# Hybrid decoder layer, one core: value sums of sparse attention in another matmul form, the C matrix of S5 in another bank, x's second read later in the queue

## What is computed

```
for block n of 128 tokens:
    p_cmp = softmax(q @ k_cmp^T ...);     o_cmp = p_cmp @ v_cmp          # 63 compressed blocks
    idx = top_k(sum of p_cmp over heads and overlaps)                    # from the ungated p_cmp
    p = softmax(q @ k_sel^T ...);         o_sel = p @ v_sel
    p = softmax(q @ k_win^T ...);         o_win = p @ v_win              # window of 512
    o = g[..., 0:1] * o_cmp + g[..., 1:2] * o_sel + g[..., 2:3] * o_win
s5:   bu = B u;  states = scan;  y = Re(C states) + D u;  gelu, glu
stick-breaking attention (4 heads)
merged = gate0 * (o_a @ w_br_nsa) + gate1 * (o_b @ w_br_s5) + gate2 * (o_c @ w_br_sb)
x = x + merged @ w_out
x = x + conv_ffn(rms_norm(x), w_up, conv_w, conv_b, w_down)
```

## Time and profile before

| what | us |
|---|---|
| median of 3 runs (1495.3 to 1495.51) | 1495.47 |
| the profiled execution | 1493.83 |
| its span | 1492.1 |
| PE busy in it | 1416.8 (95%) |
| VectorE busy | 673.0 (45%) |
| ScalarE busy | 355.2 (24%) |
| GpSimd busy | 471.1 (32%) |

### The profile page before, as it was taken

One profiled execution on the slowest core, in us unless ns is written; L12 is line 12 of the kernel. 1 busy time (PEld: TensorE's weight loads), 2 busy tenths in 40 slices (PEclk: granted clock), 3 DMA queues, 4 the chain that ended last, 5 costly groups with the idle time before them and its releaser, 6 DMA issues.

```text
span 1492.1 us, 18380 instructions
## 1 busy us (share of the span) xinstructions
PE 1416.8 (95%) x7437; PEld 1159.1 (78%) x7437; DVE 673.0 (45%) x1053; ACT 355.2 (24%) x621; POOL 471.1 (32%) x240
## 2 busy tenths in 40 slices
PE   5799799999999899999999979999999999999998
PEld 4688467799887667777778868788888888888887
DVE  5896665525453553444445231532323232364641
ACT  5311544400101134344401010421111111231110
POOL 4324002234622110111133333334434343444542
PEclk9999999999989899999999999999999999999999
DMA  7411101031101000000012041321111111141122
GB/s 181 45 29 42 43 1 29 15 76 54 36 19 52 15 22 1 19 18 18 1 36 53 29 159 53 127 72 43 49 49 42 56 42 56 42 156 56 43 72 98
DMA packets 126821, 76.44 MB, mean 51 GB/s; under 512 B 39312, under 2 KB 113424, under 8 KB 126736
## 3 DMA queue, kind: packets, MB, share of 16 engines
q1 hardware_dynamic: 126752, 75.46, 18.0%
HBM read 66.93 MB, written 8.52 MB: 51 GB/s over the span
## 4 chain that ended last, share of the span: by engine, by line
PE 88%; DVE 5%; ACT 3%; issue 1%; DMA 1%; POOL 0%; SPq 0%; ACTq 0%; DVEq 0%; POOLq 0%
PE ps L642 23%; PE ps L643 23%; PE ps L644 23%; PE ps L1123 4%; PE ps L1153 3%; PE ps L1137 2%; PE ps L875 1%; PE ps L892 1%; PE ps L905 1%; DMA raw<-in_w_out 1%; PE ps L657 1%; PE ps L1081 1%; ACT arena L1269 1%; PE ps L1100 1%; DVE hTl L2009 1%
## 5 line engine op out<-in xcount | busy, mean ns | idle before, releaser
L554 POOL TENSOR_TENSOR wh<-raw,zero 128x1024 fp32r<-128x1024 f32 (+2 forms) x93 | 188.1, 2022 | 988.3 <-PE ps L644 950.4
L642 PE MATMUL ps<-hTh,wh 128*128 128x512 f32 x1008 | 402.8, 400 | 3.9 <-ACT arena L1344 3.1
L643 PE MATMUL ps<-hTl,wh 128*128 128x512 f32 x1008 | 395.8, 393 | 0.0
L644 PE MATMUL ps<-hTh,wl 128*128 128x512 f32 x1008 | 395.6, 392 | 0.0
L557 POOL TENSOR_TENSOR wl<-raw,wh 128x1024 fp32r<-128x1024 f32 (+2 forms) x93 | 257.0, 2763 | 7.3
L642 PEld LDWEIGHTS ps<-hTh,wh 128*128 128x128 f32 x1008 | 191.7, 190 | 43.4 <-ACT arena L1344 3.5
L644 PEld LDWEIGHTS ps<-hTh,wl 128*128 128x128 f32 x1008 | 191.1, 190 | 41.1
L643 PEld LDWEIGHTS ps<-hTl,wh 128*128 128x128 f32 x1008 | 191.7, 190 | 37.8
L642 PE MATMUL ps<-wh,hTh 128*128 128x512 f32 (+2 forms) x512 | 179.9, 351 | 7.5 <-POOL wl L557 7.5
L643 PE MATMUL ps<-wl,hTh 128*128 128x512 f32 (+2 forms) x512 | 179.6, 351 | 0.0
L644 PE MATMUL ps<-wh,hTl 128*128 128x512 f32 (+2 forms) x512 | 179.5, 351 | 0.0
(11 more groups left out here) (331 smaller groups left out, 1596.7 us busy)
## 6 DMA issues: line engine op xcount, KB each, us to landing
raw<-in_w_in SPq DMA_DIRECT2D x35, 512.0 KB, 3.9
raw<-in_w_up SPq DMA_DIRECT2D x32, 512.0 KB, 4.0
raw<-in_w_down SPq DMA_DIRECT2D x16, 512.0 KB, 3.7
merged<-in_x SPq DMA_DIRECT2D x8, 512.0 KB, 7.2
raw<-in_w_out SPq DMA_DIRECT2D x8, 512.0 KB, 3.7
merged<-in_x SPq DMA_DIRECT2D x2, 2048.0 KB, 10.3
x_keep<-merged SPq DMA_DIRECT2D x2, 2048.0 KB, 10.1
conv<-x_keep SPq DMA_DIRECT2D x1, 2048.0 KB, 8.1
```

Of the source, the lines that this page charges most:

```text
L554: eng.tensor_tensor(wh[:, p, 0:n], raw[:, p, 0:n], zero1[:, 0:1].broadcast_to((P, n)), ALU.add).then_inc(s_hi[0], 1)
L642: mm(out_, ah, bh, start=first, stop=False, skip_group_check=True)
L643: mm(out_, ah, bl, start=False, stop=False, skip_group_check=True)
L644: return mm(out_, al, bh, start=False, stop=last, skip_group_check=True)
```

## The change

It has three parts.

1. **Value sums.** `pv` and `pvc` have the values stationary (128 rows by 64 columns) and stream the transposed weights, two heads on the two column halves of PE. The output comes out transposed, straight as `mixT` wants it, so `o` has no transposes. A denominator per query can't be applied to columns afterwards, so it is applied to the weights: ScalarE's `exp` also writes the row's sum (`accum_out`), and a new entry `scale` (lag 2 behind the row's last piece) has VectorE add the pieces' sums, take the reciprocal, multiply by the gate and scale the row in `prow` in place. `tp` waits for `p_scaled` of its row instead of `p_exp`. `pv` is done at the odd head's piece, for it and its partner's, with four `pT` slots in place of two. In the compressed part the gate is multiplied into the weights, behind the reduction, and `pc_ready` is sent after that.
2. **C matrix.** It goes through bank 0. Its transposes wait for the fifth `main_free`, panel 4 waits for `cT_read`, `u_transposes` no longer do.
3. **x's second read** stands at `p == P_OUT + 3`.

```diff
@@ plan
-        LAG_EXP, LAG_T, LAG_PV, LAG_OUT = 1, 3, 4, 5
+        LAG_EXP, LAG_SCALE, LAG_T, LAG_PV, LAG_OUT = 1, 2, 3, 4, 5
             if i - LAG_EXP in ROW_END:
                 PLAN.append(("exp", ROW_END[i - LAG_EXP]))
+            if i - LAG_SCALE in ROW_END:
+                PLAN.append(("scale", ROW_END[i - LAG_SCALE]))
             if 0 <= i - LAG_T < NPC:
                 PLAN.append(("tp", i - LAG_T))
-            if 0 <= i - LAG_PV < NPC:
+            if i - LAG_PV in PV_EVEN:
                 PLAN.append(("pv", i - LAG_PV))
@@ SyncE
-                if p == P_OUT + 1:
+                if p == P_OUT + 3:
@@ PE, S5
                 eng.wait_ge(S("cpack_ready"), 1)
+                eng.wait_ge(S("main_free"), 5)
-                    ins = eng.transpose(ps[:, 4, k * P:(k + 1) * P], cpack[k // 2][:, (k % 2) * P:(k % 2 + 1) * P],
+                    ins = eng.transpose(ps[:, 0, k * P:(k + 1) * P], cpack[k // 2][:, (k % 2) * P:(k % 2 + 1) * P],
@@ proj
+                    if m == 8:
+                        eng.wait_ge(S("cT_read"), 2)
@@ u_transposes
-                eng.wait_ge(S("cT_read"), 2)
@@ PE, pvc
-                        ins = mm(ps[:, 3, c0:c0 + HD], pcT[n % 2][0:N_CMP, h * P:(h + 1) * P],
-                                 vcmp[0:N_CMP, 0:HD], start=True, stop=True, skip_group_check=True)
+                        r = slice(HD * (h % 2), HD * (h % 2) + HD)
+                        ins = mm(ps[r, 3, h // 2 * P:(h // 2 + 1) * P], vcmp[0:N_CMP, 0:HD],
+                                 pcT[n % 2][0:N_CMP, h * P:(h + 1) * P], start=True, stop=True, skip_group_check=True)
@@ PE, tp
-                    eng.wait_ge(S("p_exp"), n + 1)
+                    eng.wait_ge(S("p_scaled"), row + 1)
@@ PE, pv
                     for i in range(nb):
-                        ins = mm(ps[:, 7 if v % 2 else 3, h * 65:(h + 1) * 65], pT[n % 2][:, i * P:(i + 1) * P],
-                                 kv_tok[:, kb + i, vc:vc + 65], start=h == 0 and off == 0 and i == 0,
-                                 stop=kb + i == m, skip_group_check=True)
+                        for e, piece in enumerate((PV_EVEN[n], n)):
+                            ins = mm(ps[HD * e:HD * e + HD, out_bank[m % 2], h // 2 * P:(h // 2 + 1) * P],
+                                     kv_tok[:, kb + i, vc:vc + HD], pT_block(piece % 4, i), ...
-                elif kind == "o":
-                        ins = eng.transpose(ps[:, 1, c * P:(c + 1) * P], oacc[:, n, c * P:(c + 1) * P], ident[:, :])
@@ ScalarE, exp
-                                           bias=neg_max[:, n % 8:n % 8 + 1]).then_inc(S("p_exp"), 1)
+                                           bias=neg_max[:, n % 8:n % 8 + 1], accum_out=den[:, d:d + 1]
+                                           ).then_inc(S("p_exp"), 1)
@@ VectorE, compressed
-                ins.then_inc(S("pc_ready"), 1)
-                eng.wait_ge(S("pc_ready"), hb + 1)
+                then(ins)
                 then(eng.tensor_reduce(php[:, :, 1:1 + N_CMP], pcmp.rearrange("p n h c -> p n c h"), AX.X, ALU.add))
+                for i in range(4):
+                    ins = tt(pcmp[:, i], pcmp[:, i], over(gates[:, 4 * hb + i, 0:12:3].unsqueeze(2), (P, NH, N_CMP)), ALU.mult)
+                ins.then_inc(S("pc_ready"), 1)
@@ VectorE, branches: branch_out goes
+            def scale_row(row):
+                m, br, h, end = ROWS[row]
+                d, k = den[:, 2 * (row % 4):2 * (row % 4) + 2], row % 4
+                one, r, c = d[:, 0:1], rden[:, k:k + 1], coef[:, k:k + 1]
+                eng.wait_ge(S("p_exp"), end + 1)
+                if PIECES[end][3]:
+                    then(tt(one, d[:, 0:1], d[:, 1:2], ALU.add))
+                then(eng.reciprocal(r, one))
+                g = 3 * h + (1 if br == "sel" else 2)
+                then(tt(c, r, gates[:, m, g:g + 1], ALU.mult))
+                w = (PIECES[end][3] + PIECES[end][2]) * P
+                ts(prow[row % 2][:, 0:w], prow[row % 2][:, 0:w], c, None, ALU.mult).then_inc(S("p_scaled"), 1)
@@ VectorE, o: the block's sums are added to mixT once
+                    tt(mixT[:, :, t], mixT[:, :, t], ps[:, out_bank[n % 2], 0:2 * P].rearrange("p (c q) -> p c q", c=2),
+                       ALU.add).then_inc(S("on_read"), 1)
```

More of the change, by code:

```diff
@@ L325, in program @@
         ROW_END = {end: row for row, (n, br, h, end) in enumerate(ROWS)}
-        V_END = {end: (n, br) for n, br, h, end in ROWS if h == NH - 1}
+        PARTNER = {(ROWS[row][:3], kb): i for i, (row, kb, nb, off) in enumerate(PIECES)}
+        PV_OPS = [i for i, (row, *rest) in enumerate(PIECES) if ROWS[row][2] % 2]
+        PV_EVEN = {i: PARTNER[ROWS[PIECES[i][0]][:2] + (ROWS[PIECES[i][0]][2] - 1,), PIECES[i][1]] for i in PV_OPS}
+        PV_COUNT = {}
+        for count, i in enumerate(PV_OPS):
+            PV_COUNT[i] = PV_COUNT[PV_EVEN[i]] = count + 1
+        N_END = {end: n for n, br, h, end in ROWS if h == NH - 1 and br == "sel"}
         FILLS = 100
@@ L1948, in row_max @@
                     ins.then_inc(S("max_ready"), 1)
-            def branch_out(n, br):
-                v = 2 * n + (br == "sel")
-                src = ps[:, 7 if v % 2 else 3, 0:4 * 65].rearrange("p (h d) -> p h d", h=NH)
-                one, d0 = (64, 0) if br == "sel" else (0, 1)
-                eng.wait_ge(S("pv_nsa"), {v: i for i, v in V_END.items()}[(n, br)] + 1)
-                then(eng.reciprocal(rden, src[:, :, one:one + 1].rearrange("p h o -> p (h o)")))
-                then(tt(coef, rden, gates[:, n, (1 if br == "sel" else 2):12:3], ALU.mult))
-                for h in range(NH):
-                    o = oacc[:, n, h * HD:(h + 1) * HD]
-                    ins = stt(o, src[:, h, d0:d0 + HD], coef[:, h:h + 1], o, ALU.mult, ALU.add)
-                ins.then_inc(S("on_read"), 1)
-                eng.wait_ge(S("on_read"), v + 1)
+            def scale_row(row):
[10 more added lines that the diff above has]
+                ts(prow[row % 2][:, 0:w], prow[row % 2][:, 0:w], c, None, ALU.mult).then_inc(S("p_scaled"), 1)
             for op in PLAN:
```

97 lines of the change are left out of this document (47 added, 50 removed).

## The result

The changed kernel takes 1587.81 us (median of four runs, 1587.46 to 1589.00) against 1495.49 for the kernel before beside it: a ratio of 1.061, 95% interval 1.059 to 1.063. It is slower by 92 us. I had forecast slower by 41.5, 1537 us, and the time lies above the range.

The account below looks back on a forecast made before the run. PE, busy 95% of the span, was taken to bound the kernel. Terms -10.0 - 9.25 - 19.7 - 2.5 - 6.0 + 1 + 64 + 11 + 13 = +41.5 gave 1537 us; range 1506 to 1572.

Parts of the forecast that it names:

- x: -9.25 forecast: Output panels: x's read behind the fourth panel removes a 7.65 us wait and 1.6 of slow matmuls, minus 9.25.
- the 64 and 11 forecast: Two-piece rows: PE idle for VectorE's scaling chain, plus 64; merges and GpSimd's splits falling on it, plus 11.
- The compressed part: Compressed branch: new value sums save some 4 over eight groups, gate ahead of transposes loses 1.5, minus 2.5.
- The third rival: Value sums: column halves don't run side by side, some 0.14 a matmul, +17 for -19.7, 1573 us; chance 0.02.
- so the whole 10.0 arrives: Before the stick-breaking part: PE 10.0 us earlier still leaves VectorE 3.8 us of its 13.82 wait; minus 10.0.
- the fourth rival: Early parts: C's 10.0 eaten by VectorE, or x's 9.25 by the panel behind x: 1546 to 1556; chance 0.06.
- 480 by 0.041: Value sums: 480 matmuls at 0.064 us each in place of 0.105, minus 19.7.
- 28.2: Branches: gains summed from value sums 19.7, output transposes 6.0 and compressed part 2.5.
- The clock: 13, with an end of 51: Two-piece rows: a quarter of 32 idle times, 8 by 1.6 us, lose clock, plus 13; ends 0 and 51.
- The first rival: Two-piece rows: clock falls behind nearly all 32 idle times, 51 in place of 13, 1575 us; chance 0.15.
- The one wait of 2.16 us without a fall: PE's wait at 146.29 us, its 32 following matmuls at the upper clock level, 3.79 us.
- 64, 11 and 1: Scaling apart from clock: two-piece rows' idle time 64, merges and splits 11, the first 32 one-piece rows 1.

Follow-up runs that it names:

- new forms without scaling: Changed kernel with rows neither normalised nor gated, transposes waiting for the exps alone: 1475.68 us.
- held-back splits: Kernel before with C's bank and x's read, GpSimd's splits of panels 8 and 9 held until VectorE has the S5 states: 1474.79 us, ratio 0.986.
- the work spread: Changed kernel without scaling, its 42 background products given only to steps without value sums: 1459.81 us.
- the filled idle time: Changed kernel with overwritten 128x512 products on PE before the wait for the scaled row, in two-piece rows: 1602.79 us with four, 1565.54 with two.
- short splits: Kernel before with GpSimd's splits of panels 5 to 9 cut to their last 260 columns: 1484.99 us with C's bank, 1496.02 without.
- a step later: Changed kernel with two-piece rows' transposes at lag 4, all rows' value sums at 5 and output at 6: 1493.05 us.
- another order in the same step: Changed kernel with VectorE's scaling of a row written ahead of the same step's score maximum: 1536.12 us.

## Why the prediction was wrong

The runs let each term be priced. Against the kernel before of the first sitting, 1495.3: C -2.7, x -10.0, new forms without scaling -6.9, scaling +112.1; the sum is +92.5, the measured difference, as it must be, since each is taken from the next kernel in a row.

**What held.** What bounds the kernel, and the direction. x: -9.25 forecast, -10.0 measured. The mechanism that decides: VectorE's chain between two neighbouring instructions of PE, with waits of 73.5 us for the 64 and 11 forecast. The compressed part, -3.2 for -2.5 (a gain of 3.1 behind the stick-breaking part is 6.3 where the branches start, 519.10 instead of 525.43; this is read from one profile of each, and that point lies between 518.4 and 522.0 in kernels that are equal up to it). The third rival, slow column halves, is ruled out: 1.09 us for sixteen.

**The C matrix: the step "so the whole 10.0 arrives" failed.** I took VectorE's work up to 132 us as something that doesn't move. But it lay between GpSimd's splits, which wait for PE, and PE was just what moved. The term was worth 2.7, the fourth rival's way; held-back splits return 7.8.

**The value sums: "480 by 0.041" is right as a rate and wrong as a gain.** I priced the matmuls and not the step that they leave behind. The old value sums stood in every step between two transposes and covered ScalarE's copy of the one bank; the paired ones stand in every second step. I had read the pairing in the change and not asked what it uncovers. 6.9 for 28.2; 22.8 with the work spread.

**The clock: 13, with an end of 51.** I took a quarter of the idle times at 1.6 us each. It was 30 to 36 in the two-piece rows, by the filled idle time, and at least 3.7 in the one-piece rows. The first rival, to which I gave 0.15, was at work, at some two thirds of its price: its sign, a granted clock under 0.9, is there at 0.85. The one wait of 2.16 us without a fall, which I held against it, was a weak witness. The same wait at the same place is followed by the lower level in four other kernels, for the 32 matmuls that took 3.79 us: 5.42 in both kernels with short splits, 5.80 and 6.01 in the two with held splits. The row of the kernel before with short splits:

```profile
145.82 5.42 PE L820 MATMUL ps<-merged 128*128 128x128 f32 x32
```

One row of one trace could not tell how often the clock falls.

**The scaling apart from the clock** was sized well: 112.1 less 34 to 40 leaves 72 to 78, for 64, 11 and 1. Part of it was in the wrong place: the first 32 rows lose 10.5 us, not 1. And in the 73.5 us of waits two small errors cancel: the 28 plain rows came to 51 us for 56 of the 64, and the four rows at a merge and a split to 22, for the other 8 and the 11.

Together: C 7 too much, value sums and their companions 21, scaling with its clock 23 too little (112 for 89, nearly all of it clock); less 1 for x. That is the 51 us by which the time lies above the forecast. The first two errors have one form: I priced the instructions that move and took the work beside them as given.

## What to carry to other kernels

When work is moved or made shorter, list the engines whose start hangs on it, and look what they run beside: an earlier transfer or split is work in a new place. When work is taken out from between two uses of one bank, ask what it was covering. Idle time on PE that comes back at every step costs clock besides (here 30 to 36 us for 73.5 us of waits); put distance between producer and consumer (a step later brought 95 us, another order in the same step 52) before shortening the chain.

## What the runs showed of the hardware

- GpSimd's instructions of 2.3 to 3.3 us on SBUF held a VectorE instruction that started beside them to their own end, down to one column: 0.16 became 2.64. Held were products, sums and scans with two SBUF sources, and products with one source of 8 columns and more (128x8: 0.16 became 2.27 in the kernel before; 128x128: 0.29 became 2.46). Never held were maxima read from PSUM (693 ns at most) and one-column steps with a scalar operand (217 ns at most), though they stood beside the same splits. The Trainium skill's page SBUF — State Buffer (SBUF: two separate sides) states that VectorE and GpSimd share a pair of ports as an exclusive lock, which also takes a VectorE instruction with two SBUF inputs; the trace agrees.
- PE's clock fell behind idle times of 1.6 to 2.2 us that returned every 6 to 12 us, though not behind each, and was kept up by work whose result nobody reads: 0.85, 0.95 and 1.00 with no, two and four products in the idle time. Behind one and the same idle time of 2.16 us it fell in four kernels and not in a fifth.
- The two heads' value sums on column halves ran at 0.064 us a matmul in both places. The Trainium skill's page TensorEngine Tiling (Feature Incompatibilities) rules out fast weight load for column tiles; its price does not show here.
